# Re-dealing products, early fetched rows and fetch issues among the stages of a routing and scatter loop

## The chip, the cores and the metric

The kernel runs on one core of one Trainium2 chip. Its metric is the device time of one execution in microseconds (us); lower is better. Five engines run their own instruction streams in order and wait for each other by semaphores: PE (TensorE, matrix products), DVE (VectorE), ACT (ScalarE), POOL (GpSimd) and SP (SyncE, which here only issues DMAs).

## The reference

Two transformer layers, one after the other, on 512 tokens of width 1024. The change lies in the feed-forward part of the first, a mixture over 16384 experts:

```python
q = (xb @ wq).reshape(C, PEER_HEADS, 2, PEER_DK_HALF)
s = jnp.einsum('chpd,hpnd->chpn', q, keys)
sv, si = lax.top_k(s, K)                       # 16 of 128 keys, twice per head
cand = sv[:, :, 0, :, None] + sv[:, :, 1, None, :]
top_s, sel = lax.top_k(cand..., K)             # 16 experts per head
g = jax.nn.softmax(top_s, axis=-1)
u = u_tab[eidx]
act = gelu(einsum('chkd,cd->chk', u, xb))
w = g * act
out = einsum('chk,chkd->cd', w, v_tab[eidx])
```

All is float32. 8 heads times 16 experts makes 128 experts for each token.

## The kernel before

The kernel treats the experts in two ways. For the first 128 tokens (`FETCH`) it fetches the chosen rows of `u_tab` and `v_tab` by an indirect DMA, one row per token at a time, and DVE multiplies and sums it. One such step on DVE is called a **pick** here (line 2370, one 128x1024 operation and a short read of its accumulator). For the remaining tokens it computes all experts densely: products of `u_tab` with the tokens, Gelu, multiplication by a dense matrix of gates (zero where an expert was not chosen), products with `v_tab`.

A product is 8 **k-steps** of three matmuls over 368 tokens (lines 921 to 923), since each float32 weight tile is split into a high part (`wh`, cast by ACT, line 1330) and a low part (`wl`, subtracted by POOL, line 2712). 72 of the dense products (9 groups of 8) are done while routing still runs; their Gelu (line 1609, ACT, into `tmp`) is **spilled** to DRAM (`a_scratch`). One of these is called a spilled product. It fills PE while DVE is busy with routing.

The stage around the change is written out by `drive_routing`, which each engine calls with its own functions, so that all engines walk the same list of steps:

- **Ahead**: routing of token blocks 0 and 1 (`route(0)`, `route(1)`), 13 steps each, with one spilled product each and some more, and picks on DVE once the experts of the first 128 tokens are known. At the end PE transposes the chosen indices and gates of the block (`ijg`, line 893), ACT copies them to `ijgT` (line 1574).
- **Blocks 1, 2 and 3** (`tt` in the code): 14, 16 and 16 steps of **scatter**. A step puts the gates of 8 tokens into their dense matrices: DVE compares an iota with the indices and makes one-hot matrices (`hots`, `below_XL`, `sq`, lines 2317 and 2327), ACT multiplies one of them by the gates (8 operations, line 1582), PE multiplies them (16 matmul records, line 902), ACT copies the result (line 1594). DVE and the gating ACT work one step ahead of PE. Between scatters, PE does spilled products, k-step by k-step (`ahead`), DVE does the routing of the next block (blocks 1 and 2 only, 26 pieces of unequal length) and the picks, ACT the casts and Gelus, POOL the low parts and the issues of the fetches.

Within a step each engine's order is: spilled product (ACT: cast, Gelu; POOL: low part), scatter, pick, routing pieces. How many products and picks have been done after each step is a linear share, rounded down, of the numbers for the block. Early picks are 42 of the 128; they use three buffers (`fetched0` to `fetched2`). POOL issues fetches at the place of a pick in its own stream:

```python
if before is not None:
    pool.wait_ge(*picked.at(*ROWS[before]))
```

where `before` is the row three earlier, which used the same buffer.

PE takes a bank of PSUM for each product: `b = n % 4` for the early ones, `n % 2` later, since the scatters use banks 2 and 3.

Of the kernel before, what the change touches and what calls it, by code (L numbers as in the profile page):

```python
# [48 lines left out]
EARLY_PICKS, LEAD, NEARLY, NFETCH = 42, 4, 3, 6  # L49
# [93 lines left out]
def build_program(nc, hT, wstream, gains, consts, trig, w_uq, w_ukv, keys, w_uk, w_uv, w_rg, u_rows, v_rows, out):  # L143
# [345 lines left out]
    def tensor(pe):  # L489
# [418 lines left out]
        def spill_steps():  # L908
            for n in range(SPILLED * 8):
                pe.wait_ge(*w_hi.at(tile[0]))  # L910
                pe.wait_ge(*low_of(tile[0]))
                b = n % 4 if n < 30 else n % 2
                take(b, (gelued, ("spill", n)))
                bank_of["spill", n] = banks[b]
                w1s, w2s = wh[tile[0] % NSPLIT], wl[tile[0] % NSPLIT]
                for k in range(KT):
                    if n == 0:
                        for sig, event in ffn_ready(k):
                            pe.wait_ge(*sig.at(event))
                    o, c = banks[b][:, EXTRA:REST], k * 128  # L920
                    pe.matmul(o, w1s[:, c:c + 128], XH[:, k, FETCH + EXTRA:S], start=k == 0, stop=False)  # L921
                    pe.matmul(o, w1s[:, c:c + 128], XL[:, k, FETCH + EXTRA:S], start=False, stop=False)  # L922
                    mm = pe.matmul(o, w2s[:, c:c + 128], XH[:, k, FETCH + EXTRA:S], start=False, stop=k == KT - 1)  # L923
                    if k == KT - 1:
                        mm.then_inc(*gemm.tell(("spill", n), ("tile", tile[0])))
                        tile[0] += 1
                        spilled[0] += 1
                    stepped[0] += 1
                    yield
# [351 lines left out]
    def drive_routing(route, spill, spilled, scatter, pick, ahead=None):  # L1281

        for tt in range(2):
            steps = route(tt)
            for n in range(13):
                for _ in range(2):
                    next(steps, None)
                spill()
                if tt == 1 and n > 2:
                    pick()  # L1290
                if tt == 1 and n % 3 == 2:
                    spill()
            for _ in steps:
                pass
        picks = 10
        for tt in range(1, 4):
            steps = route(tt + 1) if tt < 3 else iter(())
            done = 0
            begin = EXTRA // 8 if tt == 1 else 0
            for n in range(begin, 16):  # L1300
                base, count = ((30, 15), (45, 14), (59, 13))[tt - 1]
                now, whole = n + 1 - begin, 16 - begin
                if n == 15:
                    if ahead:
                        ahead(min(KT * base + KT * count * (2 * whole - 1) // (2 * whole), KT * spilled[0] + KT - 1))
                    for _ in steps:
                        pass
                while spilled[0] < base + count * now // whole:
                    spill()
                if ahead:  # L1310
                    ahead(KT * base + KT * count * now // whole)
                scatter((tt - 1) * 128 + n * 8)
                while picks < (10, 18, 26)[tt - 1] + (8, 8, 16)[tt - 1] * now // whole:
                    pick()
                    picks += 1
                while done < ROUTE_STEPS * now // (whole - 1):
                    next(steps, None)
                    done += 1
# [1389 lines left out]
    def gpsimd(pool):  # L2708
# [113 lines left out]
        def fetch(upto):  # L2822

            while rows[0] < min(upto, len(ROWS)):
                row = rows[0]
                what, s = ROWS[row]
                buf, before = buffer_of(row)
                if row == EARLY_PICKS + NEARLY:
                    pool.wait_ge(*scat_mm.at(REST // 4 - 1))
                    for i in range(2):  # L2830
                        pool.wait_ge(*st_g[i].at(BLOCKS - 2 + i))
                if row == 0:
                    pool.wait_ge(*routed.at(0, "experts"))
                if before is not None:
                    pool.wait_ge(*picked.at(*ROWS[before]))
                if (what, s) == ("u2", 0):
                    pool.wait_ge(*routed.at(1, "experts"))
                pool.indirect_dma_start(fetched[buf][:, :], None, u_rows if what in ("u", "u2") else v_rows,  # L2838
                                        bass.IndirectOffsetOnAxis(ap=(eidx if what in ("u", "v") else eidx2)[:, s:s + 1],
                                                                  axis=0)).then_inc(  # L2840
                                            *ld_row[buf].tell(row))
                rows[0] += 1

        def pick():
            made[0] += 1
            fetch(min(made[0] + 3, EARLY_PICKS))

        drive_routing(route, spill, spilled, scatter, pick)

# [295 lines left out]
```

## Time and profile before

| | before |
|---|---|
| median of 3 runs | 2061.41 us (2059.48 to 2063.76) |
| profiled execution | 2062.45 us, of which the span of instructions 2060.7 us |
| PE busy | 2020.1 us (98% of the span) |
| DVE, ACT, POOL busy | 1509.1, 994.8, 1048.8 us |
| mean granted clock of TensorE | 0.996 of full |
| place of the stage | Ahead: 305 to 431 us; block 1: 431 to 522 us; block 2: 522 to 618 us; block 3: 618 to 704 us |

The time of an execution is its span and 1.75 us around it. Busy time is what an engine spent in instructions; idle time of an engine matters only where PE, which is busy nearly throughout, waits in the end. The places of the blocks are read from the transposes (line 893), which stand at 431.2, 521.9 and 618.7 us.

### The profile page before, as it was taken

What the parts mean: (1) busy time and instruction counts of PE and PEld (TensorE: products, weight loads), DVE (VectorE), ACT (ScalarE), POOL (GpSimd) and SP (SyncE); (2) the same over time, 40 slices, a digit from 0 to 9 for tenths busy, and PEclk for the clock granted to TensorE, in tenths of its full rate; (3) what the DMA queues carried; (4) which work ended last, traced back from release to release, by engine and by line L of the source; (5) the groups of instructions that cost most, each with busy time, mean ns of one, the idle gap of its engine ahead of it and who ended that gap; (6) DMA issues with size and microseconds to landing.
All of it is one profiled execution on the core that took longest, in us unless ns stands there. A gap on an engine that the chain in (4) does not pass through costs nothing.

```text
span 2060.7 us, 31764 instructions
## 1 busy us (share of the span) xinstructions
PE 2020.1 (98%) x11815; PEld 1805.1 (88%) x11815; DVE 1509.1 (73%) x2840; ACT 994.8 (48%) x1825; POOL 1048.8 (51%) x615
## 2 busy tenths in 40 slices
PE   9999999999999999999999999999999999999998
PEld 8746889998999999999999999999867787877777
DVE  6237548979898478889999999997687635067763
ACT  4337433367789743333333333334556652256643
POOL 3212456764455577776766677674334444411242
PEclk9999999999999999999999999999999999999999
DMA  5330225776678899999999999996312222210021
GB/s 204 80 100 12 82 83 167 249 248 228 223 252 300 307 355 370 367 371 375 351 362 364 371 385 386 360 390 225 116 68 92 82 90 104 92 42 32 21 82 62
DMA packets 150936, 435.33 MB, mean 211 GB/s; under 512 B 14464, under 2 KB 61184, under 8 KB 148992
## 3 DMA queue, kind: packets, MB, share of 16 engines
q1 hardware_dynamic: 109312, 282.29, 39.2%
q0 software_dynamic: 41472, 151.01, 19.5%
q8 instruction: 96, 1.57, 0.3%
q14 instruction: 56, 0.46, 0.1%
HBM read 391.28 MB, written 41.97 MB: 210 GB/s over the span
## 4 chain that ended last, share of the span: by engine, by line
PE 77%; DVE 13%; issue 4%; DMA 3%; ACT 2%; POOL 1%; SPq 0%; DVEq 0%; ACTq 0%
PE bank L515 15%; PE bank L516 15%; PE bank L517 15%; PE bank L921 4%; PE bank L922 4%; PE bank L923 4%; DVE wide L2390 4%; PE bank L902 3%; DMA wraw<-in_wstream 2%; PE bank L1142 2%; PE bank L690 1%; DVE WTL L1917 1%; DVE fetched L2370 1%; PE wide L1165 1%; PE wide L1153 1%
## 5 line engine op out<-in xcount | busy, mean ns | idle before, releaser
L2712 POOL TENSOR_TENSOR wl<-wraw,wh 128x1024 fp32r<-128x1024 f32 x272 | 674.4, 2483 | 721.9 <-ACT wh L1330 720.2
L1330 ACT CAST wh<-wraw 128x1024 fp32r<-128x1024 f32 x360 | 374.7, 1045 | 179.5 <-PE bank L517 126.2
L515 PE MATMUL bank<-WTH,wh 128*128 128x368 f32 x1024 | 338.8, 331 | 11.8 <-issue 11.1
L515 PE MATMUL bank<-XH,wh 128*128 128x368 f32 (+2 forms) x976 | 344.6, 353 | 1.8 <-ACT wh L1330 1.1
L516 PE MATMUL bank<-XL,wh 128*128 128x368 f32 (+2 forms) x976 | 340.9, 349 | 0.0
L517 PE MATMUL bank<-XH,wl 128*128 128x368 f32 (+2 forms) x976 | 339.5, 348 | 0.0
L517 PE MATMUL bank<-WTH,wl 128*128 128x368 f32 x1024 | 337.5, 330 | 0.0
L516 PE MATMUL bank<-WTL,wh 128*128 128x368 f32 x1024 | 337.4, 329 | 0.0
L515 PEld LDWEIGHTS bank<-WTH,wh 128*128 128x128 f32 x1024 | 193.0, 188 | 16.2 <-issue 15.0
L921 PE MATMUL bank<-XH,wh 128*128 128x368 f32 x576 | 196.4, 341 | 8.5 <-issue 3.6
L515 PEld LDWEIGHTS bank<-XH,wh 128*128 128x128 f32 x976 | 183.4, 188 | 24.2 <-issue 4.8
L516 PEld LDWEIGHTS bank<-XL,wh 128*128 128x128 f32 x976 | 183.2, 188 | 18.4 <-issue 2.2
L517 PEld LDWEIGHTS bank<-XH,wl 128*128 128x128 f32 x976 | 183.5, 188 | 16.5
L2838 POOL DMA_INDIRECT fetched<-in_u_rows,diag x144 | 160.5, 1115 | 65.2 <-DVE fetched L2370 39.8
L516 PEld LDWEIGHTS bank<-WTL,wh 128*128 128x128 f32 x1024 | 193.0, 188 | 0.0
L517 PEld LDWEIGHTS bank<-WTH,wl 128*128 128x128 f32 x1024 | 192.9, 188 | 0.0
L922 PE MATMUL bank<-XL,wh 128*128 128x368 f32 x576 | 191.6, 333 | 0.0
L923 PE MATMUL bank<-XH,wl 128*128 128x368 f32 x576 | 191.1, 332 | 0.0
L2838 POOL DMA_INDIRECT fetched<-in_v_rows,diag x144 | 151.1, 1049 | 38.9 <-issue 29.9
L2390 DVE SCALAR_TENSOR_TENSOR wide<-fetched,diag,wide 128x1024 f32<-128x1024 f32 x127 | 162.8, 1282 | 7.3 <-DMA fetched<-in_v_rows,diag 3.3
L921 PEld LDWEIGHTS bank<-XH,wh 128*128 128x128 f32 x576 | 109.4, 190 | 11.7 <-issue 10.7
L1917 DVE TENSOR_TENSOR wl<-wraw,wh 128x1024 fp32r<-128x1024 f32 (+1 forms) x92 | 110.2, 1198 | 7.0 <-ACT wh L1330 6.5
(552 smaller groups left out, 3857.3 us busy)
## 6 DMA issues: line engine op xcount, KB each, us to landing
wraw<-in_wstream SPq DMA_DIRECT2D x360, 512.0 KB, 5.4
g_scratch<-gs SPq DMA_DIRECT2D x12, 2048.0 KB, 7.9
gr<-g_scratch SPq DMA_DIRECT2D x15, 1536.0 KB, 14.1
a_scratch<-tmp SPq DMA_DIRECT2D x72, 184.0 KB, 2.7
tmp<-a_scratch SPq DMA_DIRECT2D x46, 184.0 KB, 7.9
sq<-a_scratch SPq DMA_DIRECT2D x26, 184.0 KB, 8.8
shifted<-hc_scratch SPq DMA_DIRECT2D x12, 270.0 KB, 4.8
fetched<-in_u_rows,diag POOLq DMA_INDIRECT x144, 7.7
```

The lines of the kernel that those rows point to most:

```text
L515: pe.matmul(o, w1, x1, start=n == 0, stop=False)
L516: pe.matmul(o, w1, x2, start=False, stop=False)
L517: m = pe.matmul(o, w2, x1, start=False, stop=n == len(ks) - 1)
L902: mm = pe.matmul(bank[:, i * 128:i * 128 + 128], hots[q % 4][1][:, i, :], hots[q % 4][0][:, i, :], start=True, stop=True, skip_group_check ...
L921: pe.matmul(o, w1s[:, c:c + 128], XH[:, k, FETCH + EXTRA:S], start=k == 0, stop=False)
L922: pe.matmul(o, w1s[:, c:c + 128], XL[:, k, FETCH + EXTRA:S], start=False, stop=False)
L923: mm = pe.matmul(o, w2s[:, c:c + 128], XH[:, k, FETCH + EXTRA:S], start=False, stop=k == KT - 1)
L1330: act.copy(wh[n % NSPLIT][:, :], wraw[n % NRAW][:, :]).then_inc(*w_hi.tell(n))
L1917: return dve.tensor_tensor(lo, src, hi.bitcast(F32), ALU.subtract)
L2390: dve.scalar_tensor_tensor(wide[1][:, :], flat, eweight[:, s:s + 1], wide[1][:, :], ALU.mult, ALU.add).then_inc(*picked.tell(("v", s)))
L2712: return pool.tensor_tensor(lo, src, hi.bitcast(F32), ALU.subtract)
L2838: pool.indirect_dma_start(fetched[buf][:, :], None, u_rows if what in ("u", "u2") else v_rows, bass.IndirectOffsetOnAxis(ap=(eidx if what ...
```

## The change

Five numbers change. Ahead of the scatters 29 products are spilled instead of 30, then 16, 16 and 11 in the three blocks instead of 15, 14 and 13 (72 in both). Picks: 9 ahead instead of 10, then 6, 6 and 21 instead of 8, 8 and 16 (42 in both). At a pick, POOL issues the fetch of the row two after it instead of three after it. The extra products of the second routing stand at steps 2, 6 and 10 instead of 2, 5, 8 and 11.

```diff
@@ tensor: banks of the spilled products
-                b = n % 4 if n < 30 else n % 2
+                b = n % 4 if n < 29 else n % 2
@@ drive_routing
-                if tt == 1 and n > 2:
+                if tt == 1 and n > 3:
                     pick()
-                if tt == 1 and n % 3 == 2:
+                if tt == 1 and n in (2, 6, 10):
                     spill()
...
-        picks = 10
+        picks = 9
...
-                base, count = ((30, 15), (45, 14), (59, 13))[tt - 1]
+                base, count = ((29, 16), (45, 16), (61, 11))[tt - 1]
...
-                while picks < (10, 18, 26)[tt - 1] + (8, 8, 16)[tt - 1] * now // whole:
+                while picks < (9, 15, 21)[tt - 1] + (6, 6, 21)[tt - 1] * now // whole:
@@ gpsimd
         def pick():
             made[0] += 1
-            fetch(min(made[0] + 3, EARLY_PICKS))
+            fetch(min(made[0] + 2, EARLY_PICKS))
```

The bank of product 29 is the same by either rule (29 % 4 and 29 % 2 are both 1). No instruction is added or removed on PE, ACT or SP; all engines do the same work in another order.

DVE in block 1, in its late steps: `hots`, `below_XL` and `sq` are one-hot matrices of two steps, lines 2279 and 2286 are long pieces of the routing of the next block, line 2370 is a pick.

```order
 L2327 TENSOR_TENSOR hots<-wide,ijgT 128x1024 x2
+L2370 SCALAR_TENSOR_TENSOR fetched,diag<-fetched,below_XH 128x1024
 L2279 TENSOR_TENSOR spare<-selu,sie 128x2048
 L2286 TENSOR_REDUCE ijg<-spare 128x128
 L2327 TENSOR_TENSOR below_XL<-wide,ijgT 128x8x128
 L2317 TENSOR_TENSOR sq<-wide,ijgT 128x512 x2
-L2370 SCALAR_TENSOR_TENSOR fetched,diag<-fetched,below_XH 128x1024
 L2279 TENSOR_TENSOR spare<-selu,sie 128x2048
 L2327 TENSOR_TENSOR hots<-wide,ijgT 128x1024 x2
+L2370 SCALAR_TENSOR_TENSOR fetched,diag<-fetched,below_XH 128x1024
 L2286 TENSOR_REDUCE ijg<-spare 128x128
```

A pick has moved from behind one pair of one-hot matrices to ahead of it, and another to behind the next pair. Earlier in the block two picks have left the order altogether.

DVE in block 3, three steps in a row, before:

```order
L2370 SCALAR_TENSOR_TENSOR fetched,diag<-fetched,below_XH 128x1024
L2327 TENSOR_TENSOR hots<-wide,ijgT 128x1024 x2
L2370 SCALAR_TENSOR_TENSOR fetched,diag<-fetched,below_XH 128x1024
L2327 TENSOR_TENSOR below_XL<-wide,ijgT 128x8x128
L2317 TENSOR_TENSOR sq<-wide,ijgT 128x512 x2
L2370 SCALAR_TENSOR_TENSOR fetched,diag<-fetched,below_XH 128x1024
```

And with the change, around the first step of block 3 that has two picks:

```order
L2370 SCALAR_TENSOR_TENSOR fetched,diag<-fetched,below_XH 128x1024
L2327 TENSOR_TENSOR hots<-wide,ijgT 128x1024 x2
L2370 SCALAR_TENSOR_TENSOR fetched,diag<-fetched,below_XH 128x1024 x2
L2327 TENSOR_TENSOR below_XL<-wide,ijgT 128x8x128
L2317 TENSOR_TENSOR sq<-wide,ijgT 128x512 x2
L2370 SCALAR_TENSOR_TENSOR fetched,diag<-fetched,below_XH 128x1024
```

Every third step has two picks one behind the other (steps 3, 6, 9, 12 and 15 of 0 to 15), where each had one.

POOL in block 3, before; `wl` is the low part of a weight tile, the DMA is a fetch:

```order
L2838 DMA fetched<-in_u_rows,diag 128x1024 x2
L2712 TENSOR_TENSOR wl<-wraw,wh 128x1024
L2838 DMA fetched<-in_u_rows,diag 128x1024
L2712 TENSOR_TENSOR wl<-wraw,wh 128x1024
L2838 DMA fetched<-in_u_rows,diag 128x1024
```

POOL at the like place of block 3, with the change:

```order
L2712 TENSOR_TENSOR wl<-wraw,wh 128x1024
L2838 DMA fetched<-in_u_rows,diag 128x1024 x3
L2712 TENSOR_TENSOR wl<-wraw,wh 128x1024
L2838 DMA fetched<-in_u_rows,diag 128x1024
L2712 TENSOR_TENSOR wl<-wraw,wh 128x1024
L2838 DMA fetched<-in_u_rows,diag 128x1024 x3
```

Two low parts now stand to four fetches; the three in a row are that of the step ahead of a step with two picks, and the two of that step, which has no product.

## Rows read from the trace of the kernel before

**Rows 1.** The page, busy time of PE over the whole span.

```profile
PE 2020.1 (98%) x11815; PEld 1805.1 (88%) x11815; DVE 1509.1 (73%) x2840; ACT 994.8 (48%) x1825; POOL 1048.8 (51%) x615
```

**Rows 2.** Waits of PE, 425 to 710 us: total us, times, longest us.

```profile
PE bank L921 <- issue: 3.6, 4, 2.6
PE bank L921 <- ACT ijgT L1574: 2.6, 1, 2.6
PE bank L921 <- POOL wl L2712: 1.9, 1, 1.9
PE bank L902 <- ACT hots L1582: 0.9, 1, 0.9
```

**Rows 3.** Stages: length, busy us (instructions) per engine, PE clock, DMA share, GB/s.

```profile
369.00:432.00 63.00, 63.00 (x387) 62.62 (x386) 51.72 (x182) 24.68 (x35) 53.81 (x25) 1.00 0.79 262
432.00:530.00 98.00, 89.72 (x595) 87.73 (x594) 89.29 (x264) 71.25 (x172) 44.62 (x24) 0.97 0.64 218
530.00:620.00 90.00, 88.71 (x629) 87.37 (x629) 86.01 (x266) 74.75 (x184) 41.17 (x22) 1.00 0.71 252
620.00:706.00 86.00, 85.60 (x600) 85.05 (x599) 66.96 (x75) 77.86 (x199) 49.49 (x28) 1.00 0.83 300
```

**Rows 4.** Timeline of DVE where block 1 begins: start, us, [idle before].

```profile
432.37 2.35 DVE L2327 TENSOR_TENSOR hots<-wide,ijgT 128x1024 f32<-128x1024 f32 x2 [5.56 <-ACT ijgT L1574]
```

**Rows 5.** Timeline of ACT, then of POOL, 500 to 515 us.

```profile
500.40 2.45 ACT L1582 ACTIVATE hots<-hots,ijgT 128x128 f32<-128x128 f32 x8 [2.81 <-DVE hots L2327]
...
503.87 2.36 POOL L2712 TENSOR_TENSOR wl<-wraw,wh 128x1024 fp32r<-128x1024 f32 x1 [6.38 <-ACT wh L1330]
509.75 2.76 POOL L2838 DMA_INDIRECT fetched<-in_u_rows,diag  x1 [3.53 <-DVE fetched L2370]
512.53 2.36 POOL L2712 TENSOR_TENSOR wl<-wraw,wh 128x1024 fp32r<-128x1024 f32 x1
```

**Rows 6.** Timeline of PE, 520 to 526 us, the end of block 1.

```profile
520.14 1.95 PE L902 MATMUL bank<-hots 128*128 128x128 f32 x16
521.93 0.49 PE L893 MATMUL bank<-cst,ijg 128*128 128x128 f32 x3
...
525.56 0.41 PE L921 MATMUL bank<-XH,wh 128*128 128x368 f32 x1 [2.64 <-ACT ijgT L1574]
```

**Rows 7.** Short stages with a lower clock, columns as in rows 3.

```profile
516.30:519.80 3.50, 3.50 (x13) 3.50 (x12) 2.78 (x6) 3.31 (x5) 1.87 (x1) 0.51 0.32 128
...
526.50:530.00 3.50, 3.50 (x13) 3.50 (x12) 3.50 (x4) 1.17 (x2) 3.50 (x2) 0.51 0.24 66
```

**Rows 8.** Timeline of one step of block 3: PE, ACT, DVE, POOL.

```profile
682.25 1.05 PE L902 MATMUL bank<-below_XL 128*128 128x128 f32 x8
...
684.72 2.46 ACT L1582 ACTIVATE hots<-hots,ijgT 128x128 f32<-128x128 f32 x8
687.08 1.03 ACT L1330 CAST wh<-wraw 128x1024 fp32r<-128x1024 f32 x1
...
683.35 1.23 DVE L2327 TENSOR_TENSOR below_XL<-wide,ijgT 128x1024 f32<-128x1024 f32 x1 [1.82 <-PE bank L902]
...
685.68 1.21 DVE L2370 SCALAR_TENSOR_TENSOR fetched<-fetched,below_XH 128x1024 f32<-128x1024 f32 x1
...
682.87 2.39 POOL L2712 TENSOR_TENSOR wl<-wraw,wh 128x1024 fp32r<-128x1024 f32 x1 [4.87 <-ACT wh L1330]
685.41 0.95 POOL L2838 DMA_INDIRECT fetched<-in_u_rows,diag  x1
```

**Rows 9.** Fetches (line 2838) of 620 to 706 us, issue to landing.

```profile
DMA to landing us min/median/max: 5.1/7.2/10.6
```

**Rows 10.** Timeline of POOL and DVE, 647 to 651 us.

```profile
647.24 2.39 POOL L2712 TENSOR_TENSOR wl<-wraw,wh 128x1024 fp32r<-128x1024 f32 x1 [0.62 <-ACT wh L1330]
...
647.66 3.06 DVE L2370 SCALAR_TENSOR_TENSOR fetched<-fetched,below_XH 128x1024 f32<-128x1024 f32 x1
```

**Rows 11.** Groups by line, 620 to 706 us: busy us, mean ns, idle before.

```profile
L2370 DVE SCALAR_TENSOR_TENSOR fetched<-fetched,below_XH 128x1024 f32<-128x1024 f32 x17 | 28.3, 1665 | 1.2 <-DMA fetched<-in_u_rows,diag 1.2
```

## The prediction

> **What bounds the kernel now.** I read the page first: PE is busy for 98% of the span [rows 1]. Its work is the same after the change, so the time can only move by PE's waits and by its clock. Then the table of stages: in the last of routing block 1 all 63 us are PE's; in 432 to 530 us PE lacks 8.3 us and its mean clock is 0.97; in the two stages after it lacks 1.3 and 0.4 us [rows 3]. What is to be won lies in block 1, and what can be lost in block 3, where nothing is lost now.
>
> The list of waits gives the places: issue 3.6, `ijgT` 2.6, `wl` 1.9 and the first one-hot matrices 0.9 us, 9.0 us in all [rows 2]. "Issue" names nobody; the timelines do. At 500.4 us ACT had waited 2.81 us for DVE's one-hot matrices; its cast stands behind them, POOL's `wl` came at 503.87 after 6.38 us of waiting for that cast, and PE stood for the 1.9 us until it was done at 506.2. The next stall, 2.6 us, ends at 515 with the `wl` of 512.53, which stood behind a fetch that had waited 3.53 us for DVE's pick and then took 2.76 us [rows 5]. So both come from DVE, 89.3 of 98 us busy there [rows 3], once by way of ACT and once by way of POOL's wait for a pick. The third stall, 2.64 us before 525.56, is another thing: PE has transposed the indices at 521.93 and needs that bank back, and ACT copies it out only behind its gating [rows 6].
>
> The clock: in 516.3 to 519.8 and 526.5 to 530.0 us the granted clock is 0.51, the lower level of 1.2 GHz, each time behind one of these stalls, and PE gets 13 matmuls done in 3.5 us [rows 7]. At 2.4 GHz 387 instructions take 63 us, 0.163 us each [rows 3], so 3.5 us hold 21: each spell costs 8 x 0.163 = 1.3 us.
>
> **Prices.** A k-step is 3 matmuls, 0.49 us, a product 3.9 us. A scatter is 1.8 us (520.14 to 521.93) [rows 6]. A pick is 1.2 us alone [rows 8].
>
> **Block 1, the gain.** Take the one-hot matrices for the 13th of steps 0 to 15 (the first of rows 5). Until then DVE made 5 picks and now makes 3 (8 x 9/14 and 6 x 9/14, rounded down): 2.4 us less. PE has 8 x 16 x 11/14 = 100 k-steps ahead of it instead of 94: 3.0 us more cover. Together 5.4 us. For the next pair it is one pick and 7 k-steps, 4.6 us, for the one after two picks and 7, 5.8 us. The two stalls that these had to cover sum to 4.5 us. They should go: **-4.5**. The fetch that held up POOL waits now for the pick before the last, so that road is closed too. Neither needs a lead that DVE could not have: it doesn't wait for PE in that stretch.
>
> The first scatter has one k-step more ahead of it (8 x 16/14 = 9 instead of 8): **-0.5** of 0.9. The product less ahead of the block brings PE to the transposes 3.9 us earlier, at about 427.3. DVE then waited 5.56 us before its first one-hot matrices [rows 4], so it has 1.7 us left and a pick less to do; I cost this at nothing, and were that cover gone it would be a wait of up to 1.2 us, one pick.
>
> The third stall is a chain on ACT and PE: scatter at 520.14, copies, gating, copy of `ijgT`, PE at 525.56. PE fills it with what stands between. With the change a k-step more stands between scatter and transposes (350 instead of 351 of the 351 k-steps allowed ahead are done before): **-0.5**. About 2.1 us stay.
>
> The clock: without the first two stalls the first spell has no cause, **-1.3**. The second follows the stall that stays; I give it half, **-0.7**. In block 2 products grow from 14 to 16 and picks fall from 8 to 6, on a DVE busy 86 of 90 us; of 1.3 us lacking [rows 3] I take off **-0.7**.
>
> Sum of the gain: 4.5 + 0.5 + 0.5 + 1.3 + 0.7 + 0.7 = **8.2 us**. Bounds: 5 (half of the two stalls comes back elsewhere, the second spell stays) to 10.3 (all 9.0 of rows 2 but 2.1, both spells, 0.8 of block 2).
>
> **Block 3, the loss.** Two products less make its 16 steps 7.8 us shorter for PE: 86 - 7.8 = 78 us, the step 4.6 instead of 5.3 us (5.5 k-steps of 0.49 and 1.8, with 0.1 of change-over). ACT has 77.9 us of work less two casts and Gelus (3.0): 75. DVE has 67.0 plus 5 picks (6.0): 73 [rows 3]. All three are within 5 us of each other. Means would still let it pass; the order of the fetches does not.
>
> Count from the start of a scatter. DVE's next one-hot matrices start at +1.1 (682.25 to 683.35), its pick ends at +4.6. ACT gates from +2.5 to +4.8, then casts (687.08) [rows 8]. In a step of 4.6 us that cast falls at +0.2 of the next scatter, POOL's `wl` at +1.3 to +3.7, the fetch behind it at +3.8 (now, with 5.3 us steps, at +3.2, 685.41). It lands 5.1 to 10.6 us later, by the median 7.2 [rows 9], so at +11.0. Before, this was the row three picks on, about 14 us later; a late row cost DVE 1.2 us once in 17 picks [rows 11]. Now it is the row two picks on, and where the next step has two picks, the second of these is wanted at about +4.6. DVE may be a step late without harm: the one-hot matrices behind the picks have to be there when ACT gates the step after, at 2 x 4.6 + 2.5 = +11.7, and their first half takes 1.2 us, so the pick must end by +10.5 and start by +9.3. It starts 1.7 us too late. And in the step after, `wl` runs from +10.5 to +12.9, over the pick.
>
> That costs more than it seems. A pick that starts while `wl` runs stands until it ends: at 647.66 it took 3.06 us, until 1.0 us after the `wl` of 647.24 to 649.63 [rows 10], and the 17 picks of this stage average 1.665 us, against 1.21 alone [rows 8, 11]. So the pick ends at +14.0, the first half of the matrices at +15.2, 3.5 us late for ACT. ACT's gating has a slack of 1.3 to 1.6 us before PE (last gate wanted 1.6 us into the next scatter, at hand at +4.8 of a 4.6 us step), which leaves PE 1.9 to 2.2 us of waiting.
>
> The Trainium skill, "SBUF — State Buffer", section "SBUF: two separate sides", states it as a lock: a VectorE operation with two SBUF inputs and a GpSimd one that reads SBUF exclude each other for the whole instruction, whoever starts first. The trace agrees (3.06 us against 1.21). By that rule alone each of the 21 picks could wait a whole `wl`, 21 x 2.4 = 50 us in the worst case, and DVE would bound block 3; by the measured mean of 0.45 us a pick it is 9.5.
>
> There are four such steps inside the block (3, 6, 9, 12; after 15 nobody waits). With a landing in 5.1 us the pick is in time and nothing is lost; with 10.6 it ends at +15.6 and PE loses 3.5 to 3.8. I take 1.5 us each, a little under the middle since a late DVE also finds its next rows landed: **+6.0**. The range of it is 0 to 15.
>
> **Sum.** -8.2 + 6.0 = -2.2 us on the profiled execution's own 2062.45 us (span 2060.7 and 1.75 around it): 2060.3. That execution stands 1.0 us above the median of the runs, 2061.41, so the median becomes **2059.2**. A measurement tells changes from about 0.2%, 4.1 us, so this reads as no change.
>
> **Rivals.**
> - *The rows come in time.* DVE's lateness in block 3 is absorbed by its step of lead. For it: the shortest landing, 5.1 us [rows 9], is in time by 0.4 us, and DVE has 5 us of room in sum. Against: the moment of the fetch hangs on ACT's cast. Then -8.2 with 0 to 1.5 of loss: 2053 to 2055. Chance 0.33.
> - *DMA and lock decide block 3; slower.* The stage moves 300 GB/s at a share of 0.83 in 86 us [rows 3]. With 21 fetches of 0.5 MB instead of 16 in 78 us and the same 2 MB gate stores, it asks for some 350. If the landing goes to 10 us, each of the four steps costs 3.5 us, and single picks are late too. It decides from a landing of about 9 us on. +14 to +16 against -8.2: 2067 to 2069. Chance 0.20.
> - *The change doesn't do what it says in block 1*: a new order of picks and pieces puts DVE late at another step, and 3 to 4 us of the stalls stay, block 3 losing as forecast: 2061 to 2064. Chance 0.10.
> - *My forecast*: -5 to +1 about 2059, chance 0.37.
>
> **How the numbers follow.** Faster by over 0.2% (under 2057.3) is the first rival and a fifth of my forecast: 0.40. Slower (over 2065.5) is the second rival and some of the third: 0.22. Within: 0.38. The range leaves out the slower half of the second rival and the far end of the first: 2051 to 2067. The likeliest case's own is 2056 to 2062.
>
> **What would show it.** Right: no wait of PE over 1 us between the first scatter and the transposes of block 1; a wait of about 2 us behind these; a clock of 1.00 around the 13th step; POOL's waits for picks gone; in block 3 waits of DVE for fetched rows, and PE waiting for ACT's gates in or behind steps 3, 6, 9 and 12. Wrong: block 3 without waits of PE (then -8), or a share of DMA near 1 and landings over 9 us there (then slower), or stalls in block 1 of the old size. A difference behind 706 us is none of my steps.

## The result: slower, and the profile after

The changed kernel takes 2070.46 us (median of 19 runs, 2065.41 to 2077.13), the kernel before on the same chips 2062.58 us (19 runs, 2057.61 to 2069.25): ratio 1.0044, 95% interval 1.0033 to 1.0055, or 7.9 us more. The prediction's 2059.2 and its range up to 2067 both missed it, on the slow side. The profiled execution took 2066.98 us, span 2065.1.

PE's work is what it was [rows 1], and it is still busy for 98% of the span:

```profile
PE 2021.4 (98%) x11815; PEld 1805.7 (87%) x11815; DVE 1529.0 (74%) x2840; ACT 995.0 (48%) x1825; POOL 1056.4 (51%) x615
```

The table of stages in the windows of [rows 3]: length, busy us (instructions) of PE, PEld, DVE, ACT, POOL, granted clock of PE, DMA share, GB/s.

```profile
369.00:432.00 63.00, 63.00 (x387) 62.54 (x385) 56.78 (x184) 24.72 (x35) 50.96 (x24) 1.00 0.74 239
432.00:530.00 98.00, 94.13 (x633) 92.65 (x632) 88.24 (x262) 74.26 (x182) 48.05 (x22) 0.97 0.63 226
530.00:620.00 90.00, 90.00 (x636) 89.49 (x635) 83.85 (x256) 75.04 (x179) 42.23 (x20) 1.00 0.66 238
620.00:706.00 86.00, 76.73 (x520) 74.88 (x519) 67.30 (x79) 69.61 (x185) 48.62 (x30) 0.98 0.83 306
```

In these windows block 1 gained 4.4 us of PE's time and block 2 1.3; block 3, in which PE had lacked 0.4 us, lacks 9.3. PE's waits from 420 to 710 us name the new road (total us, times, longest us):

```profile
PE bank L902 <- ACT hots L1582: 5.9, 3, 3.2
PE bank L921 <- ACT ijgT L1574: 2.7, 1, 2.7
PE bank L921 <- issue: 2.5, 4, 1.5
PE bank L902 <- ACT below_XL L1582: 1.5, 1, 1.5
PE bank L893 <- ACT tmp L1609: 0.6, 1, 0.6
```

Against [rows 2], `wl` and most of "issue" are gone (block 1's two stalls), and 7.4 us of waiting for ACT's gating has come, all but the first scatter's 0.45 in block 3. Its owner is DVE. Here is the costliest of block 3's stalls, in the timelines of SP (`g_scratch` is the store of finished gates, 2 MB), DVE, POOL, ACT and PE:

```profile
687.80 0.32 SPq L2956 DMA_DIRECT2D g_scratch<-gs  x1
...
689.08 1.76 POOL L2838 DMA_INDIRECT fetched<-in_u_rows,diag  x1
...
692.28 1.21 DVE L2370 SCALAR_TENSOR_TENSOR fetched<-fetched,below_XH 128x1024 f32<-128x1024 f32 x1
...
698.71 1.23 DVE L2370 SCALAR_TENSOR_TENSOR fetched<-fetched,below_XH 128x1024 f32<-128x1024 f32 x1 [5.22 <-DMA fetched<-in_u_rows,diag]
...
699.86 2.35 DVE L2327 TENSOR_TENSOR hots<-wide,ijgT 128x1024 f32<-128x1024 f32 x2
...
700.22 0.95 POOL L2838 DMA_INDIRECT fetched<-in_u_rows,diag  x1 [3.10 <-DVE fetched L2370]
...
701.12 2.45 ACT L1582 ACTIVATE hots<-hots,ijgT 128x128 f32<-128x128 f32 x8 [5.02 <-DVE hots L2327]
...
701.66 3.43 PE L902 MATMUL bank<-hots 128*128 128x128 f32 x16 [3.19 <-ACT hots L1582]
```

Read downwards: the fetch of 689.08 lands 9.6 us later, and DVE stands 5.22 us for its row; the one-hot matrices behind the pick start at 699.86, ACT had been ready for 5.02 us, PE stands 3.19 us. The next fetch (700.22) goes out only once this pick has freed its buffer; it landed at 704.54, and its own pick, at 707.99, waited for nothing. The stall of 683.58 shows the other half, the pick that stands while `wl` runs:

```profile
677.89 3.97 DVE L2370 SCALAR_TENSOR_TENSOR fetched<-fetched,below_XH 128x1024 f32<-128x1024 f32 x1 [0.72 <-DMA fetched<-in_u_rows,diag]
...
677.44 0.94 POOL L2838 DMA_INDIRECT fetched<-in_u_rows,diag  x1 [4.38 <-DVE fetched L2370]
678.40 2.37 POOL L2712 TENSOR_TENSOR wl<-wraw,wh 128x1024 fp32r<-128x1024 f32 x1
...
683.04 1.28 ACT L1582 ACTIVATE below_XL<-below_XL,ijgT 128x128 f32<-128x128 f32 x4 [4.79 <-DVE below_XL L2327]
...
683.58 1.27 PE L902 MATMUL bank<-below_XL 128*128 128x128 f32 x8 [1.47 <-ACT below_XL L1582]
```

The pick takes 3.97 us instead of 1.21 and ends 1.1 us behind the `wl`. That `wl` was itself late: it stood behind a fetch that had waited 4.38 us for DVE's pick before, and PE waited 1.5 us for it too (at 680.87). Over the stage, DVE's waits for rows, POOL's waits for picks, and the landing of the fetches (before: 1.2 us of such waits [rows 11], median 7.2 us [rows 9]):

```profile
DVE fetched L2370 <- DMA fetched<-in_u_rows,diag: 15.8, 6, 5.2
...
POOL fetched L2838 <- DVE fetched L2370: 18.5, 8, 4.4
...
DMA to landing us min/median/max: 4.1/8.1/10.7
```

The median hides which rows were late. DVE waited over 1 us for four rows of block 3, issued at 626.28, 641.69, 665.72 and 689.08 us; they landed 9.6, 10.2, 10.2 and 9.6 us later. None of them had been held back for a buffer (POOL idle for 0.1 to 0.3 us before the issue), and each was issued within 1 us of the start of a 2 MB store of gates or while it ran (625.0 to 632.2, 642.6 to 653.0, 663.7 to 673.3, 687.8 to 696.2 us). The six fetches that were in flight beside such a store for 5 us or more landed in 9.3 to 10.7 us, the other 14 in 4.1 to 9.0; in the kernel before it was 8.7 to 10.6 against 5.1 to 8.8. No run moved the stores, so that they are the cause is likely and not shown. The eight fetches whose issue did wait for a pick (the 18.5 us) all brought their row in time, to within 0.14 us; what they made late is the `wl` queued behind them.

### The profile page after: what moved, and what is told of

Same layout as the page of the kernel before. It is cut to its first block, busy times and chain, and to the rows that moved or that the text cites. A ratio compares the mean times of both kernels' runs of the same rounds, so it can differ in the third digit from the quotient of the medians.

```text
span 2065.1 us, 31764 instructions
## 1 busy us (share of the span) xinstructions
PE 2021.4 (98%) x11815; PEld 1805.7 (87%) x11815; DVE 1529.0 (74%) x2840; ACT 995.0 (48%) x1825; POOL 1056.4 (51%) x615
## 4 chain that ended last, share of the span: by engine, by line
PE 79%; DVE 9%; DMA 6%; issue 3%; ACT 2%; POOL 1%; SPq 0%; DVEq 0%; ACTq 0%
PE bank L515 16%; PE bank L516 15%; PE bank L517 15%; PE bank L921 4%; PE bank L922 4%; PE bank L923 4%; PE bank L902 3%; DMA wraw<-in_wstream 3%; DVE wide L2390 2%; PE bank L1142 2%; PE bank L690 1%; DMA fetched<-in_u_rows,diag 1%; DVE WTL L1917 1%; DVE fetched L2370 1%; PE wide L1165 1%
## 5 line engine op out<-in xcount | busy, mean ns | idle before, releaser
L516 PEld LDWEIGHTS bank<-XL,wh 128*128 128x128 f32 x976 | 183.2, 188 | 18.5 <-issue 2.2
L2838 POOL DMA_INDIRECT fetched<-in_u_rows,diag x144 | 170.3, 1183 | 52.1 <-DVE fetched L2370 25.9
```

Of the source, the lines that this page charges most:

```text
L516: pe.matmul(o, w1, x2, start=False, stop=False)
```

## The experiments

The yardstick throughout: the length of block 3 in each trace, from its transposes (the third group on line 893) to the last scatter (line 902, read as the end of its last matmul but one, in every trace alike), and the "rest" from there to the end of the span. With 13 products in the block PE needs 86.0 us (kernel before, nothing lost); with 11 it needs 7.8 less by the price of a product, 78.2. The four kernels below in which PE hardly waits there took 77.8 to 77.9, so losses reckoned from 78.2 are 0.3 to 0.4 us too small. Picks and products of the table are those of block 3; "fetch" is how many rows ahead one is issued.

| kernel | products | picks | fetch | tokens in | block 3 | rest |
|---|---|---|---|---|---|---|
| before (3 traces) | 13 | 16 | 3 | SBUF | 86.0, 86.0, 86.0 | 1356.0, 1357.1, 1354.1 |
| e2 | 13 | 16 | 2 | SBUF | 85.9 | 1355.2 |
| e4 | 13 | 21 | 3 | SBUF | 88.2 | 1351.2 |
| e3 | 11 | 16 | 3 | SBUF | 77.8 | 1356.8 |
| e10 | 11 | 16 | 2 | SBUF | 77.8 | 1355.4 |
| e1 | 11 | 21 | 3 | SBUF | 85.3 | 1355.5 |
| after (4 traces) | 11 | 21 | 2 | SBUF | 90.6, 91.0, 90.8, 93.1 | 1355.1, 1362.4, 1360.6, 1358.2 |
| e8 | 11 | 21 | 3, ahead of `wl` | SBUF | 88.1 | 1353.5 |
| e5 | 11 | 21 | 2 | PSUM | 87.8 | 1359.4 |
| e6 | 11 | 21 | 3 | PSUM | 81.0 | 1354.2 |
| e7 | 11 | 16 | 3 | PSUM | 77.9 | 1360.0 |
| e9 | 11 | 19 | 3 | PSUM | 77.9 | 1352.0 |

Most of these rows rest on one trace. Where nothing is lost the traces agree (86.0 three times); where something is, they differ: 90.6 to 93.1 for the changed kernel. And a profiled execution need not be a typical one: that of the changed kernel stands 3.5 us below its median, that of e5 4.9 and of e7 4.7 above theirs, that of e4 5.1 below. So the differences of the medians are given beside those of block 3.

**The parts of the change, one by one.** First the changed kernel with the fetch put back to three rows ahead (e1), and the kernel before with only the fetch changed (e2).

```diff
 e1, in the changed kernel
-            fetch(min(made[0] + 2, EARLY_PICKS))
+            fetch(min(made[0] + 3, EARLY_PICKS))
 e2, in the kernel before
-            fetch(min(made[0] + 3, EARLY_PICKS))
+            fetch(min(made[0] + 2, EARLY_PICKS))
```

> The changed kernel with one part undone: POOL again fetches the row three after the pick, not two. Theory A (the order of the fetches costs block 3: a row issued two picks ahead lands after it is wanted): block 3 becomes about 78 to 80 us instead of 90.5, DVE no longer waits for fetched rows there, and the time is 4 to 8 us under the kernel before, 2055 to 2059. Theory B (21 picks and 16 scatters in 78 us are too much for DVE with the lock against POOL, whoever fetches when): block 3 stays at 86 to 91 us and the time 3 to 9 us above the kernel before.

> The kernel before with only the fetches one row later. Theory A: block 3 has one pick a step and steps of 5.3 us; by the numbers of its steps a row lands about 1.8 us after DVE would want it, within DVE's lead of a step, so PE loses 0 to 1 us; block 1 may win up to 2.6 us, since POOL no longer stands for DVE's pick. Time -3 to +1 us against before. Theory B: nothing moves, within 1 us.

e1: 2062.28 us, ratio to before 1.0002 (0.9987 to 1.0018); e2: 2059.63 us, 0.9992 (0.9981 to 1.0004). The later fetch costs nothing by itself. Beside the other changes it costs 5.3 us of block 3 (90.6 to 85.3; 5.5 to 7.8 from the other three traces), and by the ratios (1.0044 and 1.0002) 8.7 us of the whole, an estimate that is good to some 4 us. e1 is no faster than before all the same: 85.3 us stand for 11 products, which lies between what its two theories had expected (78 to 80, 86 to 91). Waits of PE, DVE and POOL and the picks in e1, 618 to 712 us:

```profile
PE bank L921 <- issue: 5.7, 4, 2.6
...
DVE fetched L2370 <- DMA fetched<-in_u_rows,diag: 8.3, 4, 3.8
...
POOL fetched L2838 <- DVE fetched L2370: 31.0, 16, 3.7
...
L2370 DVE SCALAR_TENSOR_TENSOR fetched<-fetched,below_XH 128x1024 f32<-128x1024 f32 x22 | 41.6, 1906 | 8.3 <-DMA fetched<-in_u_rows,diag 8.3
```

The same in e2:

```profile
DVE fetched L2370 <- DMA fetched<-in_u_rows,diag: 13.0, 5, 4.9
...
POOL fetched L2838 <- DVE fetched L2370: 1.6, 1, 1.6
```

The two settings exchange one wait for another. Two rows ahead, with a pick a step, the buffer is free when the fetch is issued (POOL waits 1.6 us in e2; 18.5 in the changed kernel), and DVE waits for the row (13.0). Three ahead, POOL issues it into a buffer that the pick has yet to free, waits 31.0 us, and each `wl` queued behind it is late; PE's "issue" of 5.7 us is that (its longest parts, 2.3 and 2.6 us, end with the `wl` of 661.9 and 678.2). In e2 these 13.0 us cost PE nothing, where 15.8 do in the changed kernel: with 16 picks in 86 us DVE has the slack for them.

Then the kernel before with the products alone (e3), the picks alone (e4), and products with the later fetch (e10).

```diff
 e3 (and e10, with the fetch of e2 as well)
-                if tt == 1 and n % 3 == 2:
+                if tt == 1 and n in (2, 6, 10):
-                base, count = ((30, 15), (45, 14), (59, 13))[tt - 1]
+                base, count = ((29, 16), (45, 16), (61, 11))[tt - 1]
 e4
-        picks = 10
+        picks = 9
-                while picks < (10, 18, 26)[tt - 1] + (8, 8, 16)[tt - 1] * now // whole:
+                while picks < (9, 15, 21)[tt - 1] + (6, 6, 21)[tt - 1] * now // whole:
```

> The kernel before with only the products moved (29, 16, 16, 11); picks and fetches as before. Theory A: block 3 with its 16 picks and early fetches holds 78 to 80 us without waits of PE over 1 us, block 1 loses its stalls in part: -3 to -7 us against before. Theory B (the short block 3 itself is at fault, by ACT and DVE having less room): block 3 at 82 to 88 us, +2 to +6 us against before.

> The kernel before with only the picks moved (9, 6, 6, 21); products and fetches as before. Theory A: block 3 stays at 86 to 87 us, since its steps are long and the rows early; block 1 wins about half of its 4.5 us: -1 to -4 us against before. Theory B (21 picks are too many for DVE in block 3, lock included): block 3 at 88 to 92 us, +1 to +6 us.

> The kernel before with the products moved and the fetches one row later, picks as before (16 in block 3, one a step). Theory by steps (a row is late only where a step has two picks): block 3 at 78 to 80 us, time 3 to 7 us under before, within 2 us of the products alone. Theory by landing (two rows in flight can't bring a row every 4.6 us when they land after 8): block 3 at 81 to 86 us, time within 3 us of before.

e3: 2056.87 us, 0.9975 (0.9963 to 0.9988). e4: 2059.39 us, 0.9995 (0.9981 to 1.0008). e10: 2056.48 us, 0.9982 (0.9968 to 0.9996). The products alone are worth 5 us; with the later fetch block 3 stays at 77.8, so neither of these is the loser, and e10's theory by landing (81 to 86 us) is out. The picks alone take 2.2 us in block 3 (88.2, the worse of its two theories, though the time is no longer) and give 4.3 to 5.8 in block 1 (84.9 against 89.2, 89.2 and 90.7 in the three traces of before). Block 1 shows what each part does there. Of its two stalls, by `wl` at 506 and by "issue" at 515, e2 (fetch) keeps the first, 1.92 us, e3 (products) keeps one of 2.58 and e10 (both) one of 1.58; only e4 (picks) has neither. Picks in e4 and in e3, 618 to 712 us:

```profile
L2370 DVE SCALAR_TENSOR_TENSOR fetched<-fetched,below_XH 128x1024 f32<-128x1024 f32 x22 | 47.2, 2160 | 3.9 <-DMA fetched<-in_u_rows,diag 3.9
```

```profile
L2370 DVE SCALAR_TENSOR_TENSOR fetched<-fetched,below_XH 128x1024 f32<-128x1024 f32 x17 | 38.0, 2239 | 0.0
```

A mean pick of 2.2 us, 1 us of it standing behind `wl`, harms nobody in e3: with 16 picks DVE has the time. Products less and picks more together are what block 3 does not hold: 0, +2.2 alone (e3, e4), +7.1 together (e1), +12.4 with the later fetch (after).

**The lock by itself.** A pick reads the row and the tokens, both in SBUF, and so stands while POOL's `wl` runs. Late in the kernel before, picks read the tokens from PSUM. e5 is the changed kernel with the tokens in PSUM from the second pick of block 3 on; e6 is e5 with the fetch of e1; e7 is e3 with it (TOKENS_FROM 27).

```diff
+TOKENS_FROM = 22
 ACT, scatter, at its end (moved here from behind drive_routing)
+            if t0 == 256:
+                for half in range(2):
+                    act.wait_ge(*routed.at(3, "replaced", half))
+                act.copy(wide[0][:, :].rearrange("p (k d) -> p k d", k=KT), xtok).then_inc(*xtok_out.tell("psum"))
 DVE, pick
-            early = made[0] < EARLY_PICKS
+            early = made[0] < TOKENS_FROM
```

> The changed kernel, but from the second step of block 3 the picks read the tokens from PSUM instead of SBUF (ACT's copy of the tokens to PSUM, 1.0 us, moves from behind block 3 into its first step). A pick then has one SBUF input, and the 86 later picks of this form took at most 1.22 us in both traces. Theory L (the lock between picks and POOL's low parts makes the larger part of the loss): picks of block 3 at 1.21 us each, block 3 at 80 to 84 us instead of 90.6, time 6 to 10 us under the changed kernel. Theory F (late landing of the rows makes it): picks at 1.21 us all the same, but DVE waits for rows 15 us or more, block 3 at 87 to 90 us, 0 to 4 us under the changed kernel.

> The changed kernel with fetches three rows ahead and with the tokens in PSUM in block 3. Theory L: POOL waits less for picks (they are short now) and block 3 comes to 78 to 80 us, near what PE's work alone takes; time 2052 to 2056, 5 to 9 us under the kernel before. If 21 picks in the short block cost by DVE's plain time and by POOL's waits for them: block 3 at 83 to 86 us, time within 3 us of before.

> The kernel before with the products moved (29, 16, 16, 11) and the tokens in PSUM from the second step of block 3. With products alone block 3 took 77.8 us and PE waited 0.7 us there, so the lock costs PE nothing in it: time as with the products alone, within 1.5 us, 4 to 7 us under before. If it is more than 2 us faster than that, the lock cost something behind block 3.

e5: 2062.84 us, 1.0013 (0.9998 to 1.0027). e6: 2053.86 us, 0.9971 (0.9959 to 0.9983). e7: 2055.28 us, 0.9968 (0.9954 to 0.9981). Block 3 is 2.8 us shorter on the changed kernel (e5; 3.0 to 5.3 from its other traces), 4.3 with the earlier fetch (e6, 85.3 to 81.0), not at all on e3 (e7). The ratios say 6.4 us for either of the first two (1.0044 to 1.0013, 1.0002 to 0.9971), again good to some 4 us. In e6, 618 to 712 us:

```profile
PE bank L922 <- issue: 3.2, 3, 2.9
...
DVE fetched L2372 <- DMA fetched<-in_u_rows,diag: 15.2, 6, 5.1
...
POOL fetched L2840 <- DVE fetched L2372: 19.5, 10, 5.4
...
L2372 DVE SCALAR_TENSOR_TENSOR fetched<-fetched,wide 128x1024 f32<-128x1024 f32 x20 | 24.1, 1214 | 15.2 <-DMA fetched<-in_u_rows,diag 15.2
```

And in e5:

```profile
PE bank L903 <- ACT hots L1583: 5.8, 2, 3.6
...
DVE fetched L2372 <- DMA fetched<-in_u_rows,diag: 25.2, 8, 6.8
```

These picks take 1.21 us each, the lock is gone, and in e5 PE still waits 5.8 us for gates while DVE waits 25.2 us for rows, more than in the changed kernel. So late rows make PE wait without any lock. Which of the two costs more is not shown: block 3 of e5 (87.8) is what its theory of late rows had expected, its median, 7.6 us under the changed kernel's, what the theory of the lock had. In e6 what is left is mainly one wait of PE, 2.9 us for the `wl` behind a fetch that had stood 5.4 us for a pick.

**A fetch ahead of `wl`.** e8 is the changed kernel where POOL, in block 3, issues the fetch before it makes the low parts.

```diff
 POOL, spill
+            if spilled[0] > 61:
+                fetch(min(made[0] + 3, EARLY_PICKS))
```

> The changed kernel, but in block 3 POOL issues the next fetch ahead of the low part of a step instead of behind it, so about 2 to 4 us earlier; the picks, the products and the lock are the same. Theory F: the rows come in time, DVE's waits for rows fall from 15.8 to under 6 us, block 3 at 83 to 87 us, time 3 to 7 us under the changed kernel. Theory L: block 3 stays at 88 to 91 us. A third way: POOL's fetch now waits for DVE's pick ahead of the low part, and PE waits for the low part instead: block 3 at 88 us or more with PE's waits at the products.

2064.0 us, 1.0015 (1.0003 to 1.0027); block 3 88.1. Waits in block 3:

```profile
PE bank L921 <- issue: 7.8, 4, 2.9
...
POOL fetched L2840 <- DVE fetched L2370: 31.2, 15, 3.9
```

It gives back 2.5 us of block 3, and by the ratios 6.0 us, by another road: the fetch waits for the pick that frees its buffer, now ahead of every `wl`, and PE stands 7.8 us at its products instead of its scatters. Issued earlier, the fetch meets the limit of three buffers, which was the third way of the expectation. A fourth was not tried.

**A version between.** e9 is e6 with 7, 7 and 19 picks (TOKENS_FROM 24).

```diff
-                while picks < (9, 15, 21)[tt - 1] + (6, 6, 21)[tt - 1] * now // whole:
+                while picks < (9, 16, 23)[tt - 1] + (7, 7, 19)[tt - 1] * now // whole:
```

> Products 29, 16, 16, 11; picks 9, 7, 7, 19; fetches three rows ahead; tokens in PSUM in block 3. If the three measured causes are all of it, block 3 takes 78 to 80 us, blocks 1 and 2 together 191 to 193, and the time is 7 to 10 us under the kernel before, 2051 to 2054. If the number of picks counts only beyond what three buffers can bring in, it is no better than the version with 21 picks (2054 to 2056).

2053.43 us (2047.89 to 2060.78), 0.9961 (0.9946 to 0.9977), the lowest median here and 17 us below the changed kernel, though its interval doesn't tell it from e3, e6, e7 and e10. Its waits from 618 to 712 us:

```profile
PE bank L922 <- issue: 0.3, 2, 0.2
...
DVE fetched L2372 <- DMA fetched<-in_u_rows,diag: 11.3, 7, 2.7
...
POOL fetched L2840 <- DVE fetched L2372: 9.2, 5, 2.9
```

and its stage inside block 3:

```profile
620.00:694.00 74.00, 73.66 (x524) 73.11 (x523) 60.08 (x77) 70.62 (x188) 42.53 (x28) 1.00 0.91 339
```

PE is full at 339 GB/s and a DMA share of 0.91, above the changed kernel's 306 and 0.83: the mean rate of the DMA engines was not the limit. Single rows land late here too (those beside a gate store in 10.2 to 11.0 us) and PE doesn't wait for them. Two picks fewer take the remaining 3.1 us away, and block 1 pays 0.9 (89.1 against 88.2).

**The part behind block 3.** The profiled pair differs by 4.4 us in span, the medians by 7.9. So both kernels were profiled again, unchanged: the changed one three times more, the one before twice more.

> The changed kernel unaltered, looked at again. Its profiled execution gained 7 us in blocks 1 and 2 and lost 12.6 us in block 3, 4.4 us in all, while its median is 8 us over that of before. Theory A: the loss of block 3 varies by how late the rows land, so another execution shows block 3 at 88 to 98 us and the other stages as they were. Theory B: the rest is lost behind block 3 (over 706 us), with block 3 at 90 to 91 us again.

> The same once more, for the spread: by theory A the span moves with the length of block 3, by theory B with the part behind it.

> The kernel before, unchanged, one more execution with its profile. What it is to tell: of the 7.9 us between the medians, the last scatter accounts for 5.3 us; the rest behind block 3 took 1356.0 us in the one trace of before and 1355.1, 1362.4 and 1360.6 us in three of the changed kernel. Theory A (the part behind block 3 varies by execution whatever the kernel): a rest between 1358 and 1362 us turns up here too, with a stall or clock spells that the first trace did not have. Theory B (the change hands a later state of the buffers to the part behind, which costs it some 4 us in most executions): 1355 to 1357 us, and no wait of PE for the low parts made by DVE of over 1 us just behind block 3. Block 3 itself 86 us by both.

> The same again. Theory A: the two rests of these looks and the first differ by over 2 us among themselves. Theory B: all three within 1355 to 1357 us.

> The changed kernel, unchanged, on the chip of the two looks at the kernel before. Theory B: block 3 91 us and a rest of 1360 to 1362 us, with a wait of PE of about 3 us for DVE's low parts at some 726 to 730 us; the span 8 us over that of the kernel before. Theory A: a rest anywhere from 1355 to 1362 us, overlapping with those of the kernel before.

The changed kernel: 2073.81, 2072.04 and 2071.26 us; the kernel before: 2062.28 and 2059.24. The last scatter ends at 710.0, 709.7, 709.6 and 711.2 us with the change and at 704.7, 703.0 and 703.1 before: the profiled execution of before was a late one, by 1.6 us. In its second and third trace the stall at 515 us was 1.1 us where it had been 2.6 [rows 2]. PE in the second trace of before:

```profile
506.19 0.41 PE L921 MATMUL bank<-XH,wh 128*128 128x368 f32 x1 [1.93 <-POOL wl L2712]
...
514.88 0.41 PE L921 MATMUL bank<-XH,wh 128*128 128x368 f32 x1 [1.07 <-issue]
```

The means of the last scatter are 710.1 and 703.6, 6.5 us apart. The rests overlap (1354.1 to 1357.1 before, 1355.1 to 1362.4 after), and three of the four after are above all of before. One place shows: PE waits for a low part that DVE makes, 0.9, 3.1 and 2.7 us in three of the four traces of the changed kernel, in none of the three before. In the second trace of the changed kernel:

```profile
728.99 0.64 PE L515 MATMUL bank<-XH,wh 128*128 128x368 f32 x1 [3.06 <-DVE WTL L1917]
```

The fourth has a rest of 1358.2 without it. In the means of these traces the rest is 3.4 us longer with the change (1359.1 against 1355.7), of 9.8 us between the spans; the medians of the 19 runs leave 1.4 us for it, 7.9 less the 6.5. Whether the change causes it or executions vary by as much is left open: the three traces of before differ by 3.0 us among themselves, e7, with 16 picks, has a rest of 1360.0, and e4, with 21, one of 1351.2.

## Why the prediction was wrong, point by point

- **Block 1's two stalls (-4.5): right.** No wait of PE over 0.2 us is left between the first scatter and the transposes (lines 902 and 893 at 432.68 and 515.44). The forecast had counted on products and picks for it; e4 shows that the picks alone do it. In the other two traces of before the two stalls are 3.0 us, not 4.5, so the usual gain is smaller.
- **The first scatter (-0.5 of 0.9): right**, 0.95 to 0.45 us.
- **The third stall (-0.5): wrong, +0.6.** It is 2.69 us, as before 2.64 [rows 6], and the transposes now wait 0.56 us for ACT as well. In e3, which keeps a stall of 2.58 us just before, the transposes wait for nothing and the third stall is 2.12 us, the half us less that was forecast. With that stall gone PE comes to ACT's chain earlier and waits for it.
- **The clock (-1.3 and -0.7): half.** The profiled execution has one spell of twice the length in place of two, behind the stall that stays, so nothing was won in it; the other three have one of 3.4 us at about 520, which is one spell less, 1.3 us. PE behind the third stall:

```profile
519.19 0.64 PE L921 MATMUL bank<-XH,wh 128*128 128x368 f32 x1 [2.69 <-ACT ijgT L1574]
```

```profile
517.70:524.50 6.80, 5.31 (x17) 5.34 (x18) 5.43 (x5) 3.60 (x8) 4.43 (x2) 0.50 0.37 127
```

- **Block 2 (-0.7): right**, 1.3 us: all 90 us of its window are PE's.
- **The gain in sum (-8.2): right within its bounds.** The transposes of block 3 stand at 619.4 us with two products more behind them than before at 618.7: 7.8 - 0.7 = 7.1 us. Against the two other traces of before (617.1) it is 5.5, and with the other three of the changed kernel (618.2 to 618.7) 6.2 to 6.7.
- **Block 3's loss (+6.0) is the step that failed.** It measures 90.6 - 78.2 = 12.4 us in the profiled trace and 12.6 to 14.9 in the others. The mechanism was the predicted one as far as it went: a row that lands too late, a pick held by `wl`, both passed on by the one-hot matrices to ACT's gates. Two of its terms failed.
- **The first is the size of a late step, "I take 1.5 us each".** PE stood in front of step 6 for 2.3 us (655.81), in front of step 11 for 3.0 (1.5 at a product at 680.87, 1.5 at 683.58) and in front of step 14 for 3.2 (701.66); with 0.8 in small waits at products that is 9.3 us in all. The places are near the forecast's, behind the double steps 3, 9 and 12; that of step 6 cost 0.6. The forecast went by the median landing, 7.2 us, and took something off, "since a late DVE also finds its next rows landed". The rows that DVE waited for had landed in 9.6 to 10.2 us, and for 10.6 the prediction itself had 3.5 to 3.8 us a step. The reason for the discount held for the rows and not for the time: the row behind a late one was waited for by 0.7 us at most in this trace (up to 2.3 in the others), but the late pick frees its buffer late, POOL waits for it (18.5 us in the block, 12.6 before, where the prediction had "POOL's waits for picks gone" and no such wait in its chain for block 3), and the `wl` behind that fetch comes late for PE and lies over the next pick, as at 678.40.
- **The second is a term that was put at nothing: PE's slower work in block 3.** Of the 12.8 us by which its block 3 is longer than that of e3, with the same 553 matmul records in it, 8.9 are waits of PE and 3.9 are matmuls that took longer: a spell of the low clock behind the last stall, and scatters that ACT's gates let through one by one (2.44 us for that of 655.81, at the full clock, where one takes 1.8). Block 3 of e3, of the changed kernel, and of its fourth trace, columns as in [rows 3]:

```profile
622.40:700.20 77.80, 77.47 (x553) 76.92 (x551) 73.95 (x76) 73.64 (x196) 40.65 (x27) 1.00 0.87 313
```

```profile
619.40:710.00 90.60, 81.33 (x553) 79.47 (x552) 70.65 (x83) 74.16 (x196) 52.51 (x33) 0.98 0.81 298
```

```profile
618.20:711.20 93.00, 84.49 (x553) 83.06 (x551) 66.26 (x83) 74.31 (x196) 52.48 (x33) 0.93 0.80 293
```

In its four traces PE waits 9.3, 8.9, 7.8 and 8.5 us in the block, at a mean clock of 0.98, 0.96, 0.94 and 0.93, with 3.4, 6.8, 10.2 and 13.7 us of the low clock; its busy time is 3.9, 4.7, 5.7 and 7.0 us above that of e3. So the executions differ by how often the clock fell behind a stall, and the forecast had a price for such a spell, 1.3 us, and did not use it here. The spell of the profiled trace:

```profile
702.00:705.40 3.40, 3.40 (x18) 3.40 (x17) 3.40 (x6) 3.40 (x10) 0.82 (x1) 0.51 0.43 149
```

- In the traces the 12.4 us come apart as 5.3 for the later fetch (90.6 to 85.3, e1), 4.3 for the lock (to 81.0, e6), and 2.8 that remain for 21 picks (to 78.2; with 19 of them nothing is lost, e9). In another order the shares differ (the lock is 2.8 if taken first, e5), and by the ratios fetch and lock are worth 8.7 and 6.4 us of the whole; the shares are rough, for the reasons given with the table. What doesn't hang on them: each part alone costs 0 or 2.2 us of the block, and all together 12.4.
- **The rivals.** "DMA and lock decide block 3; slower", with 0.20, is what happened: +14 to +16 against -8.2 was its price, 12.4 to 14.9 against -5.5 to -7.1 the measured one. Its condition came true in part: the rows that were waited for landed in 9.6 to 10.2 us, but the median landing was 8.1 and the share of DMA did not rise (0.83). Its number was partly luck, since it had no term for the clock either. "The rows come in time" and "doesn't do what it says in block 1" are refuted.
- **"A difference behind 706 us is none of my steps."** There may be one, of 1.4 or 3.4 us, open as said.

The rule of the Trainium skill that the prediction named ("SBUF — State Buffer", "SBUF: two separate sides": two SBUF inputs against a GpSimd operation that reads SBUF) holds here: with one input moved to PSUM the picks fall to 1.214 us each. With both in SBUF the order decides, as that section says: in the kernel before, the pick of 647.66, begun after its `wl`, took 3.06 us, and that of 698.60, begun 0.1 us ahead of one, took 1.22 while the `wl` took 3.40 instead of 2.4. The 3.97 us of 677.89 don't fit at first sight, since that pick began 0.5 us ahead of its `wl`; POOL was issuing a fetch then, and whether that counts as the other's turn no run tells. The worst case of 50 us would have been far off as a price: the lock measured 2.8 to 4.3 us of the block and some 6 by the ratios.

## What to carry to other kernels

Two edits that each use up slack of one engine have to be costed together, at the place where both draw on it: alone they cost 0 and 2.2 us of block 3 here, together 7.1. Reckon a transfer that must be in time by the landings of its own moment and not by the median: here the rows that cost time were those beside a 2 MB store, 9.6 to 10.2 us against a median of 8.1. Where a ring of few buffers feeds an engine, a late consumer holds up the queue that issues the next transfer, with all that is queued there behind it, and issuing earlier moves the wait to that queue (15.8 us on DVE became 31.0 on POOL). Where an engine with a clock of two levels has new stalls, add the spells behind them. Before trusting a difference of a few microseconds between two traces, profile each kernel more than once: here the first trace of before alone hid 1.6 us, and that of e5 stood 4.9 us above its median.

## What the runs showed of the hardware

- One operand in PSUM frees the pick from the lock altogether: 20 picks at a mean of 1.214 us while 16 `wl` ran in the same stretch (e6), against means of 1.44 to 2.24 with both operands in SBUF in kernels with 16 and 21 picks.
- Mean picks of 2.2 us (e3) cost nothing, and waits of DVE for rows of 13.0 us (e2) cost nothing, where one of them comes alone.
- A stage can run at 339 GB/s and a DMA share of 0.91 with PE at its full 2.4 GHz (e9), while the slower changed kernel, with the same transfers to make, moved 306: its lower mean rate goes with its stalls.
- A 0.5 MB fetch that was in flight beside a 2 MB store for 5 us or more landed in 9.3 to 10.7 us, the others in 4.1 to 9.0 (changed kernel, block 3).
- Like waits of PE are not always followed by the low clock: behind the stall at 655 us, of 2.3, 2.5, 2.4 and 2.6 us in the four traces of the changed kernel, it fell in the last three. In e8 it fell behind a wait of 2.5 us and not behind one of 2.9.
